# Sample attention of a decoder step: keys turned by VectorE in 32 by 32 blocks, scores in sixteen array tiles, pages loaded across sequences

## The chip, the core and the metric

The kernel runs on one core of a Trainium2 chip. The metric is device microseconds from launch to end, with the median of the runs as the kernel's time.

## The reference, cut to what matters

Layer 1 of the trunk attends with stick breaking. The change touches only the sample group: 8 sequences of 8 new tokens each, 16 heads of 64, and 4096 cached keys and values in 32 pages of 128 rows. A page of keys is 128 rows of 1024 fp32 numbers, 512 KB, and so is a page of values; 512 pages are read, 268 MB.

```python
def _stick_breaking(q, k, v, q_pos0, break_bias):
    ...
        z = jnp.einsum('bqhd,bkhd->bhqk', qb, kb) * scale + bias
        mask = kpos[None, :] < qpos[:, None]
        log_beta = jax.nn.log_sigmoid(z)
        log_keep = jnp.where(mask, log_beta - z, 0.0)
        rest = lax.cumsum(log_keep, axis=3, reverse=True) - log_keep
        a = jnp.where(mask, jnp.exp(log_beta + rest), 0.0)
        outs.append(jnp.einsum('bhqk,bkhd->bqhd', a, vb))
```

So each key's weight needs the sum of softplus(z) over all later keys. The kernel goes through the pages from the last to the first and subtracts that sum from z by matmuls with a triangular matrix.

## The kernel before

The program is a list of stages, each a block of its own: setup, pooling mixer, MLP, projections, `attend_sample` (the stage changed), `attend_prompt`, projection, MLP, norms. Every engine has its own in-order stream of instructions inside a stage; semaphores tie them together.

`attend_sample` first handles the 64 new keys (front part, up to the exponential of `zn` into `att_new`). Then comes a loop over the 8 sequences (`Fori(0, DB)`), with 8 units each; a unit is 4 pages. In a unit TensorE does, in this order:

1. `turn_keys(u)`: 32 transposes of 128 by 128 turn 4 pages of keys into PSUM, four banks in rotation. ScalarE and VectorE copy every other bank to `k_t` (`keep_turned`).
2. `scores(u)`: 8 matmuls, each with 32 query columns as weights and 512 keys streaming, on the four column tiles of the array. Each fp32 matmul stands in the profile as two MATMUL instructions.
3. `subtract_sums(u-1)`: 10 fp32r matmuls.
4. `turn_scores(u)`: 4 transposes of the biased scores `z_rows`, which VectorE made from the bank `Z`.
5. `values(u-1)`: 16 matmuls, on the four column tiles.

ScalarE takes abs, exp and ln of the turned scores (`t`), and later the exponential that gives the weights `att`. VectorE makes the softplus `sp` and its two fp32r halves `sp_hi`, `sp_lo`; GpSimd keeps `behind`, the sum over the pages already done. At a sequence's end the last `subtract_sums` and `values` run alone, VectorE picks each head's block of the result, and only then does the next sequence's first `scores` start.

SyncE issues the page loads in order: 4 pages of keys of unit u (two buffers of 4 pages, each waits until the page that it overwrites has been turned), then 4 pages of values of unit u-1 (8 slots, they wait on `v_used`). Its first key load waits on `k_turned`, which TensorE raises only after the new keys' part.

Of the kernel before, what the change touches and what calls it, by code (L numbers as in the profile page):

```python
# [16 lines left out]
ALU = mybir.AluOpType  # L17
ACT = mybir.ActivationFunctionType
AX = mybir.AxisListType
# [90 lines left out]
def setup(nc, k, a):  # L110
    with ExitStack() as ctx:
# [39 lines left out]
        def _(pool):  # L151
            def made_by(ins):
# [12 lines left out]
            made_by(pool.tensor_copy(k.neg_ones[:, :], k.scratch[:, :]))  # L165
# [9 lines left out]
            made_by(pool.memset(k.scratch[:, :], 0.0))  # L175
            made_by(pool.affine_select(out=k.scratch[:, :], in_=k.scratch[:, :], compare_op=ALU.is_gt, fill=MASKED,
                                       base=0, pattern=[[1, P]], channel_multiplier=-1))
            made_by(pool.tensor_copy(k.mask_diag[:, :], k.scratch[:, :]))
# [19 lines left out]
        MADE = 19 + HIST  # L198
# [752 lines left out]
def attend_sample(nc, k, a):  # L951
# [4 lines left out]

    with ExitStack() as ctx:
        o = k.HH_AT
        k_t = k.at("sa_kt", [P, NC, 512], F32, o)
        k_pages = [k.at("sa_kpage0", [P, 4, D], F32, o + 16384), k.at("sa_kpage1", [P, 4, D], F32, o + 51712)]  # L960
        z_rows = k.at("sa_zrows", [P, 512], F32, o + 32768)
        t = k.at("sa_t", [P, 512], F32, o + 34816)
        spl = k.at("sa_sp", [P, 4, P], F32, o + 36864)
        sp_hi = k.at("sa_sphi", [P, 2, 4, P], F32R, o + 38912)
        sp_lo = k.at("sa_splo", [P, 2, 4, P], F32R, o + 43008)
        behind = k.at("sa_behind", [P, P], F32, o + 47104)
        behind_hi = k.at("sa_behindhi", [P, 2, P], F32R, o + 47616)
        q_tiles = k.at("sa_q", [P, NC, 32], F32, o + 49152)
        o_part = k.at("sa_op", [P, 4, HD], F32, o + 50176)
        o = k.WORK_AT  # L970
        v_page = k.at("sa_vpage", [P, 8, D], F32, o)
        k_new = k.at("sa_knew", [P, D], F32, o + 32768)
        v_new = k.at("sa_vnew", [P, D], F32, o + 36864)
        att = k.at("sa_a", [P, 2, 512], F32, o + 40960)
        behind_lo = k.at("sa_behindlo", [P, 2, P], F32R, o + 45056)
        pages2 = k.at("sa_pages2", [P, 2, P], F32, o + 46080)
        att_new = k.at("sa_anew", [P, DB, P], F32, o + 47104)
        sp_new = k.at("sa_spnew", [P, DB, P], F32, o + 51200)
        o_rows = k.at("sa_or", [P, DB, P], F32, o + 55296)
        att_b = k.at("sa_ab", [P, P], F32, o + 59392)  # L980

        o = k.HH_AT
        zn = k.at("sa_zn", [P, DB * P], F32, o)
        spn_hi = k.at("sa_spnhi", [P, DB * P], F32R, o + 4096)
        spn_lo = k.at("sa_spnlo", [P, DB * P], F32R, o + 8192)
        tn = k.at("sa_tn", [P, DB * P], F32, o + 12288)
        kn_t = k.at("sa_knt", [P, NC, P], F32, o + 32768)
        (zeroed, kn_in, vn_in, kn_turned, kn_kept, zn_part, zn_done, zn_kept, tn_own, tn_done, dve_new, spn_done, trin_done,
         an_done, k_turned, act_kept, dve_kept, z_done, z_kept, zt_done, act_own, t_done, s_done, sp_done, behind_done,
         pool_own, tri_done, a_done, ab_done, v_used, o_row, o_turned, dve_own, q_ready) = sems(  # L990
            ctx, nc, "sa", "zeroed", "kn_in", "vn_in", "kn_turned", "kn_kept", "zn_part", "zn_done", "zn_kept", "tn_own",
            "tn_done", "dve_new", "spn_done", "trin_done", "an_done", "k_turned", "act_kept", "dve_kept", "z_done",
            "z_kept", "zt_done", "act_own", "t_done", "s_done", "sp_done", "behind_done", "pool_own", "tri_done",
            "a_done", "ab_done", "v_used", "o_row", "o_turned", "dve_own", "q_ready")
# [3 lines left out]
        UNITS = 8  # L998
        TURNS = 64
        Z, ZTS, OA = k.ps[3], [k.ps[4], k.ps[6]], k.ps[5]  # L1000
        ZN = [k.ps[5], k.ps[6]]
        OT = [k.ps[6], k.ps[3]]
        TURN_BANKS = [k.ps[0], k.ps[1], k.ps[2], k.ps[7]]
        npages = a["cache_k"].shape[0]

# [3 lines left out]
        @block.sync  # L1009
        def _(sp):  # L1010
            kc = a["cache_k"].rearrange("n p h d -> n p (h d)")
            vc = a["cache_v"].rearrange("n p h d -> n p (h d)")
            sp.wait_ge(zeroed, 2)
            sp.dma_start(k_new[0:TS, :], a["k_sample"].rearrange("b t h d -> (b t) (h d)")).then_inc(kn_in, 16)
            sp.dma_start(v_new[0:TS, :], a["v_sample"].rearrange("b t h d -> (b t) (h d)")).then_inc(vn_in, 16)
            with sp.Fori(0, DB) as b:

                page = {}
                for u in range(UNITS + 1):
                    for g in range(4 if u < UNITS else 0):  # L1020
                        n = 4 * u + g
                        page[n] = sp.value_load(k.pages[0:1, bass.ds(b * PAGES + (PAGES - 1 - n), 1)],
                                                min_val=0, max_val=npages - 1)

                        sp.wait_ge(k_turned, b * TURNS + (2 * (n + 25) if n < 8 else 2 * (n - 7) + TURNS))
                        sp.dma_start(k_pages[u % 2][:, g, :], kc[bass.ds(page[n], 1), :, :].rearrange("n p d -> (n p) d")
                                     ).then_inc(k_in[n % 8], 16)
                    for g in range(4 if u else 0):
                        n = 4 * (u - 1) + g
                        sp.wait_ge(v_used, b * UNITS + (u + 6))  # L1030
                        sp.dma_start(v_page[:, n % 8, :], vc[bass.ds(page[n], 1), :, :].rearrange("n p d -> (n p) d")
                                     ).then_inc(v_in[n % 8], 16)

        @block.gpsimd
        def _(pool):
            pool.memset(k_new[:, :], 0.0).then_inc(zeroed, 1)
            pool.memset(v_new[:, :], 0.0).then_inc(zeroed, 1)
            pool.memset(o_rows[:, :, :], 0.0).then_inc(zeroed, 1)

            own = Tally(pool, pool_own)  # L1040
            OWN = 2 + 7 * 4
            pool.wait_ge(spn_done, 1)
            pool.wait_ge(an_done, 1)
            with pool.Fori(0, DB) as b:
                own.base, own.k = b * OWN, 0
                for u in range(UNITS):
                    hi, lo = behind_hi[:, u % 2, :], behind_lo[:, u % 2, :]
                    pool.wait_ge(s_done, b * UNITS + (u + 1))
                    pool.wait_ge(behind_done, b * UNITS + u)
                    if u == 0:  # L1050
                        own.do(pool.tensor_tensor(behind[:, :], sp_new[:, bass.ds(b, 1), :].rearrange("p b n -> p (b n)"),
                                                  k.zeros[:, :], ALU.add))
                    else:
                        own.do(pool.tensor_tensor(pages2[:, :, :], spl[:, 0:2, :], spl[:, 2:4, :], ALU.add))
                        own.do(pool.tensor_tensor(pages2[:, 0, :], pages2[:, 0, :], pages2[:, 1, :], ALU.add))
                        own.do(pool.tensor_tensor(behind[:, :], behind[:, :], pages2[:, 0, :], ALU.add))
                    own.do(pool.tensor_tensor(hi, behind[:, :], k.zeros[:, :], ALU.add))
                    pool.tensor_tensor(lo, behind[:, :], hi.bitcast(F32), ALU.subtract).then_inc(behind_done, 1)
                    if u == 0:
                        pool.wait_ge(ab_done, b)  # L1060
                        pool.tensor_tensor(att_b[:, :], att_new[:, bass.ds(b, 1), :].rearrange("p b n -> p (b n)"),
                                           k.zeros[:, :], ALU.add).then_inc(ab_done, 1)
                assert own.k == OWN, own.k

        def keep_turned(eng, copy, mine, b, u, kept, pages):

            for g in pages:
                for h in range(2):
                    job = 8 * u + 2 * g + h
                    if job % 2 != mine:  # L1070
                        continue
                    eng.wait_ge(k_turned, b * TURNS + (TURNS + job + 1))
                    eng.wait_ge(z_done, b * UNITS + (u + 1))
                    copy(k_t[:, 4 * h:4 * h + 4, g * P:(g + 1) * P],
                         TURN_BANKS[job % 4][:, :].rearrange("p (c n) -> p c n", c=4)).then_inc(kept, 1)

        @block.scalar
        def _(act):
# [13 lines left out]
            act.wait_ge(an_done, 1)  # L1092
            act.sem_inc(act_kept, 32)
            with act.Fori(0, DB) as b:
# [6 lines left out]
                for u in range(UNITS):  # L1101
                    keep(u, range(4))
                    if u:
                        weights(u - 1)
# [622 lines left out]
```

## Time and profile before

| | |
|---|---|
| median of 3 runs | 3733.98 us (3733.38 to 3736.93) |
| profiled execution | 3737.79 us |
| its span | 3736.1 us |
| busy in the span | PE 86%, PE weight load 73%, DVE 50%, ACT 25%, POOL 16% |
| mean granted TensorE clock | 0.946 of 2.4 GHz |
| packets of the page loads | 4096 bytes each, 128 to a page |

The profile gives for each engine what it did and what ended its idle time. A stage is read with a view of stretches (busy time by engine, granted clock as PEclk with 1.00 for 2.4 GHz and 0.50 for 1.2 GHz, DMA rate) and with the timeline, whose rows give a start, a duration and a number of merged instructions.

### The profile page before, as it was taken

The numbers are of one execution on the slowest core, as the hardware profiler recorded it, in microseconds if no ns is written. First come the engines' busy times: TensorE is split into PE (matmuls) and PEld (weight loads), VectorE is DVE, ScalarE is ACT, GpSimd is POOL, SyncE is SP. The second block draws the span as 40 slices with busy tenths as digits, with TensorE's granted clock in tenths as the row PEclk, the third lists the DMA queues.
The fourth block names the chain that finished last, engine by engine and source line by source line (L and its number), as shares of the span: only waits on it lengthen the run. The fifth ranks groups of instructions, "written<-read, shape, count | busy, mean of one in ns | idle before, by whom it ended". The sixth has DMA issues, their size and how long they took to land. (4 is left out here: it accounts for less than half of the span.)

```text
span 3736.1 us, 57991 instructions
## 1 busy us (share of the span) xinstructions
PE 3210.8 (86%) x20912; PEld 2718.3 (73%) x20912; DVE 1885.8 (50%) x3138; ACT 937.8 (25%) x1598; POOL 610.8 (16%) x528
## 2 busy tenths in 40 slices
PE   5655999999995979788888887888885999999997
PEld 1235999999985979555555555444484999999996
DVE  2566555555543121344444444888815555555554
ACT  0113000000012010333333333777714100000003
POOL 0002222212101111122222221000010222222210
PEclk7887999999997989899999998999997999999998
DMA  8702111111101220798888886000010211111101
GB/s 323 261 29 62 46 45 45 40 43 42 39 0 58 88 63 26 284 351 341 337 350 334 340 339 225 22 19 23 6 45 0 68 45 45 45 45 45 45 22 48
DMA packets 215604, 432.70 MB, mean 116 GB/s; under 512 B 13664, under 2 KB 130057, under 8 KB 212441
## 3 DMA queue, kind: packets, MB, share of 16 engines
q1 hardware_dynamic: 215521, 431.67, 31.7%
q8 instruction: 43, 0.70, 0.1%
q14 instruction: 40, 0.33, 0.0%
HBM read 417.92 MB, written 13.92 MB: 116 GB/s over the span
## 5 line engine op out<-in xcount | busy, mean ns | idle before, releaser
L84 PE MATMUL bank<-hi,mlp_uphi 128*128 128x364 f32 (+1 forms) x1536 | 506.9, 330 | 92.2 <-POOL mlp_uplo L697 92.2
L85 PE MATMUL bank<-lo,mlp_uphi 128*128 128x364 f32 (+1 forms) x1536 | 506.7, 330 | 0.0
L86 PE MATMUL bank<-hi,mlp_uplo 128*128 128x364 f32 (+1 forms) x1536 | 506.6, 330 | 0.0
L85 PE MATMUL bank<-mlp_flo,mlp_dnhi 128*128 128x364 f32 (+1 forms) x1536 | 504.7, 329 | 0.0
L86 PE MATMUL bank<-mlp_fhi,mlp_dnlo 128*128 128x364 f32 (+1 forms) x1536 | 504.7, 329 | 0.0
L84 PE MATMUL bank<-mlp_fhi,mlp_dnhi 128*128 128x364 f32 (+1 forms) x1536 | 504.6, 329 | 0.0
L307 DVE SCALAR_TENSOR_TENSOR x_t<-bank,mod,x_t 128x364 f32<-128x364 f32 (+1 forms) x432 | 245.5, 571 | 379.7 <-PE bank L86 377.4
L84 PEld LDWEIGHTS bank<-hi,mlp_uphi 128*128 128x128 f32 x1536 | 290.5, 189 | 93.4 <-POOL mlp_uplo L697 93.4
L697 POOL TENSOR_TENSOR mlp_uplo<-mlp_raw,mlp_uphi 128x1024 fp32r<-128x1024 f32 x64 | 162.5, 2540 | 827.3 <-ACT mlp_uphi L682 423.3
L85 PEld LDWEIGHTS bank<-lo,mlp_uphi 128*128 128x128 f32 x1536 | 290.5, 189 | 0.0
L86 PEld LDWEIGHTS bank<-hi,mlp_uplo 128*128 128x128 f32 x1536 | 290.3, 189 | 0.0
L86 PEld LDWEIGHTS bank<-mlp_fhi,mlp_dnlo 128*128 128x128 f32 x1536 | 288.7, 188 | 0.0
L85 PEld LDWEIGHTS bank<-mlp_flo,mlp_dnhi 128*128 128x128 f32 x1536 | 288.7, 188 | 0.0
L84 PEld LDWEIGHTS bank<-mlp_fhi,mlp_dnhi 128*128 128x128 f32 x1536 | 288.7, 188 | 0.0
L697 POOL TENSOR_TENSOR mlp_dnlo<-mlp_raw,mlp_dnhi 128x1024 fp32r<-128x1024 f32 x64 | 163.2, 2550 | 673.7 <-ACT mlp_dnhi L682 673.7
L1249 PEld LDWEIGHTS bank<-ident,sa_kpage 128*128 128x128 f32 x2048 | 225.6, 142 | 44.6 <-issue 24.7
L1249 PE MATMUL bank<-ident,sa_kpage 128*128 128x128 f32 x2048 | 247.4, 277 | 12.0 <-ACT sa_kt L1100 6.0
L682 ACT ACTIVATE mlp_dnhi<-mlp_raw 128x1024 fp32r<-128x1024 f32 x64 | 67.4, 1053 | 750.7 <-PE bank L86 656.1
L718 DVE TENSOR_SCALAR mlp_f<-bank 128x364 f32<-128x364 f32 (+1 forms) x192 | 102.2, 532 | 234.7 <-PE bank L86 234.7
L722 DVE TENSOR_TENSOR mlp_flo<-mlp_f,mlp_fhi 128x364 fp32r<-128x364 f32 (+1 forms) x192 | 198.4, 1033 | 6.6
L682 ACT ACTIVATE mlp_uphi<-mlp_raw 128x1024 fp32r<-128x1024 f32 x60 | 63.7, 1061 | 534.5 <-PE bank L86 534.5
L84 PE MATMUL bank<-kv_hi,hi 128*128 128x256 f32 (+1 forms) x576 | 163.4, 284 | 38.1 <-POOL kv_lo L820 38.1
(255 smaller groups left out, 5652.7 us busy)
## 6 DMA issues: line engine op xcount, KB each, us to landing
sa_kpage<-in_cache_k SPq DMA_DIRECT2D x256, 512.0 KB, 6.4
sa_vpage<-in_cache_v SPq DMA_DIRECT2D x256, 512.0 KB, 6.1
mlp_raw<-in_w_up SPq DMA_DIRECT2D x64, 512.0 KB, 4.0
mlp_raw<-in_w_down SPq DMA_DIRECT2D x64, 512.0 KB, 3.5
w_raw<-in_w_ada SPq DMA_DIRECT2D x24, 1024.0 KB, 8.6
pm_wada<-in_w_ada SPq DMA_DIRECT2D x48, 512.0 KB, 5.2
kv_raw<-in_w_kv SPq DMA_DIRECT2D x8, 1024.0 KB, 5.5
x_rows<-in_x_prompt SPq DMA_DIRECT2D x1, 4096.0 KB, 13.4
```

The source lines that it names most:

```text
L84: pe.matmul(out, w_hi, x_hi, start=start, stop=False, skip_group_check=True)
L85: pe.matmul(out, w_hi, x_lo, start=False, stop=False, skip_group_check=True)
L86: return pe.matmul(out, w_lo, x_hi, start=False, stop=stop, skip_group_check=True)
L307: dve.scalar_tensor_tensor(out=x, in0=psum[:, 0:wp], scalar=g[:, 8 * gate + m, 0:1], in1=x, op0=ALU.mult, op1=ALU.add).then_inc(free, 1)
L682: act.activation(split_target(kind, c)[0], raw[:, r % 2, :], ACT.Copy).then_inc(w_hi_done, 1)
L697: pool.tensor_tensor(lo, raw[:, slot, :], hi.bitcast(F32), ALU.subtract).then_inc(w_done, 1)
L718: own.do(dve.tensor_scalar(ft, u, 0.0, None, ALU.max))
L722: dve.tensor_tensor(f_lo[:, c, c0:c0 + w], ft, hi.bitcast(F32), ALU.subtract).then_inc(bank_free, 1)
L1249: last = pe.transpose(TURN_BANKS[job % 4][:, c * P:(c + 1) * P], k_pages[u % 2][:, g, (4 * h + c) * P:(4 * h + c + 1) * P], k.ident[:, :])
```

## The change

`attend_sample` is rewritten around other units of work, and its loop over sequences is unrolled on all engines but SyncE, which loops over the first seven sequences.

- `turn_keys` moves to VectorE: one `dve.transpose` per page (128 partitions, 1024 elements) turns each 32 by 32 block in place, SBUF to SBUF. The copies on ScalarE and VectorE go.
- `scores` takes 128 matmuls of 32 rows, 32 weight columns and 128 keys, on the 16 tiles of the array, each row quarter into its own bank. The queries are laid out for this by `ready_queries`, 16 small copies per sequence on VectorE.
- ScalarE adds the bias: 4 activations of 128 columns make `z_rows`.
- `values(n-1)` stands between `scores(n+1)` and `turn_scores(n+1)`; `subtract_sums(n)` is last and has 6 matmuls in place of 10, because VectorE keeps a running sum `c_run` (4 adds of 128 columns per unit). GpSimd's part shrinks to the new keys.
- Units are numbered through the sequences (n from 0 to 63); two PSUM banks `OA` alternate between sequences, and `finish(b)` runs inside the next sequence.
- SyncE issues keys of unit n+1, then values of unit n, without a break between sequences, and the first keys may load before the new keys' part is done. In setup the constants `neg_ones` and `mask_diag` go.

The core of the diff:

```diff
+            def load_keys(b, u):
+                for g in range(4):
+                    page[4 * u + g] = page_of(b, 4 * u + g)
+                    sp.wait_ge(turned, b * (4 * UNITS) + (4 * u + g - 7 + EARLY_K))
+                    sp.dma_start(k_raw[u % 2][:, g, :], ...).then_inc(k_in[4 * (u % 2) + g], 16)
+            def load_values(b, u):
+                for g in range(4):
...
+                    sp.wait_ge(v_used, b * UNITS + (u - 1 + EARLY_V))
+                    sp.dma_start(v_page[:, 4 * (u % 2) + g, :], ...).then_inc(v_in[4 * (u % 2) + g], 16)
...
+            def softplus_of_negative(n):
+                act.wait_ge(z_done, n + 1)
+                act.wait_ge(zt_done, n)
+                for r in range(4):
+                    act.activation(z_rows[:, :, r, :],
+                                   Z[r][:, P * (n % 2):P * (n % 2) + P].rearrange("p (x j) -> p x j", j=32),
+                                   ACT.Identity, bias=k.bias_row[:, 0:1]).then_inc(z_kept, 1)
...
+            def turn_keys(n, x):
...
+                dve.wait_ge(k_in[4 * (n % 2) + x], 16 * (n // 2 + 1))
+                dve.transpose(k_t[n % 2][:, x, :], k_raw[n % 2][:, x, :]).then_inc(turned, 1)
...
+            for n in range(W):
+                dve.wait_ge(l_done, n + 1)
+                dve.scalar_tensor_tensor(flat, ZT[n % 2][:, :], 0.0, flat, ALU.max, ALU.add).then_inc(sp_done, 1)
...
+                for g in range(4):
...
+                    dve.tensor_tensor(c_run[:, g, :], before, t[:, g, :], ALU.add).then_inc(c_done, 1)
...
+                dve.tensor_copy(c_hi[:, n % 2, :, :], c_all).then_inc(hi_done, 1)
+                dve.tensor_tensor(c_lo[:, n % 2, :, :], c_all, c_hi[:, n % 2, :, :].bitcast(F32), ALU.subtract
+                                  ).then_inc(lo_done, 1)
+                for x in range(4):
+                    turn_keys(n + 2, x)
+                if u == 1 and b:
+                    finish(b - 1)
+                if 2 <= u < 6 and b + 1 < DB:
+                    ready_queries(b + 1, u - 2)
...
+            def scores(n):
+                pe.wait_ge(turned, EARLY_K + 4 * n + 4)
...
+                for hh in range(4):
+                    for half in range(2):
+                        for r in range(4):
+                            for g in range(4):
+                                d0 = HD * (4 * g + hh) + 32 * half
+                                last = pe.matmul(
+                                    Z[r][32 * g:32 * g + 32, P * (n % 2):P * (n % 2) + P].rearrange("p (x j) -> p x j", j=32),
+                                    q_w[b % 2][32 * r:32 * r + 32, g, half, 32 * hh:32 * hh + 32],
+                                    k_t[n % 2][32 * r:32 * r + 32, :, d0:d0 + 32], ...
+                                    tile_position=(32 * r, 32 * g), skip_group_check=True)
...
+            for n in range(W):
+                if n + 1 < W:
+                    scores(n + 1)
+                if n:
+                    values(n - 1)
+                if n + 1 < W:
+                    turn_scores(n + 1)
+                subtract_sums(n)
```

## Rows read from the trace of the kernel before

**Rows 1.** The page's first line.

```profile
span 3736.1 us, 57991 instructions
```

**Rows 2.** Stretches: the loop over the sequences, with the columns' names.

```profile
core 0: us, PE busy (x) PEld busy (x) DVE busy (x) ACT busy (x) POOL busy (x), PEclk, DMA share, GB/s
...
1524.40:2309.60 785.20, 657.39 (x6080) 449.23 (x6080) 343.74 (x559) 302.52 (x512) 183.28 (x312) 0.98 0.88 341
```

**Rows 3.** Timeline of one unit: start us, us, engine, line, operation [idle before].

```profile
1598.57 1.92 PE L1262 MATMUL bank<-sa_kt,sa_q 128*32 128x512 f32 x16 [1.25 <-issue]
...
1600.42 0.50 PE L1287 MATMUL bank<-sa_sphi,neg_tri 128*128 128x512 f32 x1
...
1602.26 0.60 PE L1271 MATMUL bank<-ident,sa_zrows 128*128 128x128 f32 x4
...
1603.11 1.93 PE L1294 MATMUL bank<-sa_vpage,sa_a 128*32 128x256 f32 x32 [0.25 <-ACT sa_a L1097]
...
1604.97 3.72 PE L1249 MATMUL bank<-ident,sa_kpage 128*128 128x128 f32 x32
...
1608.21 4.05 SPq L1026 DMA_DIRECT2D sa_kpage<-in_cache_k  x4
...
1609.93 1.92 PE L1262 MATMUL bank<-sa_kt,sa_q 128*32 128x512 f32 x16 [1.25 <-issue]
```

**Rows 4.** Timeline at a sequence's end and the next one's first scores.

```profile
1621.05 1.93 PE L1294 MATMUL bank<-sa_vpage,sa_a 128*32 128x256 f32 x32 [0.69 <-ACT sa_a L1097]
...
1628.30 1.92 PE L1262 MATMUL bank<-sa_kt,sa_q 128*32 128x512 f32 x16 [1.06 <-DVE sa_kt L1074]
```

**Rows 5.** Stretches: page loads saturated, setup, and the first 75 us of the loop.

```profile
1562.00:1592.00 30.00, 25.51 (x236) 17.41 (x238) 13.41 (x21) 11.49 (x20) 7.19 (x13) 1.00 1.03 408
...
50.00:70.00 20.00, 11.83 (x72) 1.81 (x68) 1.00 (x2) 0.00 (x0) 0.00 (x0) 0.82 1.01 421
...
1524.40:1600.00 75.60, 63.91 (x578) 44.53 (x578) 34.87 (x57) 30.13 (x51) 19.55 (x34) 0.97 1.01 400
```

**Rows 6.** Groups of instructions in the loop: count, busy us, mean ns, idle before.

```profile
L1180 DVE TENSOR_TENSOR sa_splo<-sa_sp,sa_sphi 128x512 fp32r<-128x512 f32 x64 | 55.8, 872 | 0.3
...
L1174 DVE SCALAR_TENSOR_TENSOR sa_sp<-bank,sa_t 128x512 f32<-128x512 f32 x64 | 44.3, 692 | 223.7 <-ACT sa_t L1112 223.7
...
L1108 ACT ACTIVATE sa_t<-bank 128x512 f32<-128x512 f32 x64 | 37.9, 592 | 34.8 <-PE bank L1271 34.8
...
L1177 DVE CAST sa_sphi<-sa_sp 128x512 fp32r<-128x512 f32 x64 | 31.9, 498 | 0.3
```

**Rows 7.** Timeline: VectorE over 1024 elements, the new keys' last softplus half.

```profile
1518.54 1.23 DVE L1130 TENSOR_TENSOR sa_spnlo<-sa_spnew,sa_spnhi 128x1024 fp32r<-128x1024 f32 x1
```

**Rows 8.** One line's instructions: VectorE's reduction over 256, ns min/median/max.

```profile
L1188 DVE TENSOR_REDUCE sa_or<-sa_op x8: 585/610/618, 1623.7 to 2310.3; 128x256 f32 x8
```

**Rows 9.** Groups over 128 columns on VectorE and ScalarE, in `attend_prompt`.

```profile
L1499 DVE TENSOR_TENSOR pa_crun<-pa_crun,pa_t 128x128 f32<-128x128 f32 x32 | 7.7, 283 | 0.0
...
L1437 ACT ACTIVATE pa_t<-bank 128x128 f32<-128x128 f32 x24 | 6.6, 275 | 3.7 <-DVE bank L1487 3.7
```

**Rows 10.** Timeline: matmuls on two row halves; weight loads for four column tiles.

```profile
2343.94 1.13 PE L1540 MATMUL bank<-q_t,pa_kt 64*128 64x512 f32 x4
...
1545.88 0.16 PEld L1294 LDWEIGHTS bank<-sa_vnew,sa_ab 128*32 128x32 f32 x8 [0.17 <-issue]
```

**Rows 11.** Stretch: the new keys' part, just before the loop.

```profile
1495.00:1524.00 29.00, 17.49 (x78) 15.00 (x78) 6.41 (x8) 4.51 (x5) 0.00 (x0) 0.50 0.10 30
```

**Rows 12.** Stretch: 200 us of `attend_prompt`, whose code is unrolled.

```profile
2400.00:2600.00 200.00, 167.56 (x792) 87.75 (x792) 169.50 (x350) 153.86 (x359) 7.62 (x8) 0.97 0.07 22
```

**Rows 13.** TensorE's code queue, 2400 to 2600, then 1545.5 to 1546.6: packets, MB, share.

```profile
q8 instruction: 6, 0.10, 0.2%
...
q8 instruction: 1, 0.02, 5.9%
```

**Rows 14.** Timeline: the stage's last instructions.

```profile
2311.61 3.52 DVE L1195 COPY o_s<-bank 64x32 f32<-64x32 f32 x32 [0.75 <-PE bank L1326]
```

More of the change, by code:

```diff
@@ L965, in attend_sample @@
[L965 to L969, printed above, removed]
+        k_raw = [k.at(f"sa_kraw{s}", [P, 4, D], F32, o + 16384 * s) for s in range(2)]
+        k_t = [k.at(f"sa_kt{s}", [P, 4, D], F32, o + 32768 + 16384 * s) for s in range(2)]
+        kn_t = k.at("sa_knt", [P, NC, P], F32, o + 32768)
@@ L1015, in _, with page_of @@
             sp.dma_start(v_new[0:TS, :], a["v_sample"].rearrange("b t h d -> (b t) (h d)")).then_inc(vn_in, 16)
-            with sp.Fori(0, DB) as b:
-                page = {}
[L1019 to L1032, printed above, removed]
+            def page_of(b, n):
+                return sp.value_load(k.pages[0:1, bass.ds(b * PAGES + (PAGES - 1 - n), 1)], min_val=0, max_val=npages - 1)
@@ new lines, in _ @@
+            page = {}
+            load_keys(0, 0)
+            with sp.Fori(0, DB - 1) as b:
+                page = {}
+                for u in range(UNITS):
+                    if u + 1 < UNITS:
+                        load_keys(b, u + 1)
+                        load_values(b, u)
+                    else:
+                        kept = dict(page)
+                        load_keys(b + 1, 0)
+                        page = kept
+                        load_values(b, u)
+            page = {}
@@ L1034, in _ @@
+            for u in range(UNITS):
+                if u + 1 < UNITS:
+                    load_keys(DB - 1, u + 1)
+                load_values(DB - 1, u)
         @block.gpsimd
@@ L1037, in _ @@
             pool.memset(v_new[:, :], 0.0).then_inc(zeroed, 1)
[L1038 to L1075, printed above, removed]
+            for s in range(2):
+                pool.memset(q_w[s][:, :, :, :], 0.0).then_inc(q_zeroed, 1)
@@ L1130, in _, with ready_queries @@
             dve.tensor_tensor(spn_lo[:, :], sp_flat, spn_hi[:, :].bitcast(F32), ALU.subtract).then_inc(spn_done, 1)
+            dve.tensor_reduce(sp_all[:, :], sp_new[:, :, :].rearrange("p b n -> p n b"), AX.X, ALU.add).then_inc(summed, 1)
+            def ready_queries(b, g):
+                if b == 0 and g == 0:
+                    dve.wait_ge(q_zeroed, 2)
+                if b >= 2:
+                    dve.wait_ge(z_done, UNITS * (b - 1))
+                rows = slice(32 * g, 32 * g + 32)
+                for par in range(2):
+                    for half in range(2):
+                        src = 64 * par + 32 * half
+                        dve.tensor_copy(
+                            q_w[b % 2][rows, :, half, :].rearrange("p g (h s) -> p g h s", h=4)[:, :, par::2, 0:DS],
+                            k.q_t[src:src + 32, :, TP + b * DS:TP + b * DS + DS].rearrange("p (g r) q -> p g r q", r=2)
+                            ).then_inc(q_ready, 1)
+            for g in range(4):
+                ready_queries(0, g)
             dve.wait_ge(trin_done, 1)
@@ new lines, in turn_scores, with subtract_sums @@
+            def turn_scores(n):
+                pe.wait_ge(z_kept, 4 * n + 4)
+                if n >= 2:
+                    pe.wait_ge(a_done, n - 1)
+                for x in range(4):
+                    last = pe.matmul(ZT[n % 2][:, P * x:P * x + P], z_rows[:, x, :, :].rearrange("p r j -> p (r j)"),
+                                     k.ident[:, :], start=(x == 0), stop=False, is_transpose=True, skip_group_check=True)
+                last.then_inc(zt_done, 1)
+            def subtract_sums(n):
+                b, u = divmod(n, UNITS)
+                zt = ZT[n % 2][:, :].rearrange("p (g n) -> p g n", g=4)
+                pe.wait_ge(lo_done, n + 1)
+                if u == 0:
+                    pe.wait_ge(new_ready, 2 * b + 1)
+                for half, new in ((c_hi, pn_hi), (c_lo, pn_lo)):
+                    pe.matmul(zt, k.neg_tri[:, :], half[:, n % 2, :, :], start=False, stop=False, skip_group_check=True)
+                    pe.matmul(zt[:, 1:4, :], k.neg_above[:, :], half[:, n % 2, 0:3, :], start=False, stop=False,
+                              skip_group_check=True)
+                    last = pe.matmul(zt[:, 0, :], k.neg_above[:, :], half[:, 1 - n % 2, 3, :] if u else new[:, :],
+                                     start=False, stop=(half is c_lo), skip_group_check=True)
+                last.then_inc(tri_done, 1)
@@ new lines, in add_values, with values @@
+            def add_values(b, weight, v, start, stop):
+                for q in range(4):
+                    last = pe.matmul(OA[b % 2][32 * q:32 * q + 32, 0:4 * HD], weight[:, 32 * q:32 * q + 32],
+                                     v[:, 256 * q:256 * q + 256], start=start, stop=stop,
+                                     tile_position=(0, 32 * q), skip_group_check=True)
+                return last
+            def values(n):
+                b, u = divmod(n, UNITS)
+                if u == 0:
+                    pe.wait_ge(new_ready, 2 * b + 2)
+                    pe.wait_ge(vn_in, 16)
+                    if b >= 2:
+                        pe.wait_ge(o_part_done, b - 1)
+                    add_values(b, att_b, v_new, True, False)
+                pe.wait_ge(a_done, n + 1)
+                for g in range(4):
+                    slot = 4 * (n % 2) + g
+                    pe.wait_ge(v_in[slot], 16 * (n // 2 + 1))
+                    last = add_values(b, att[:, g, :], v_page[:, slot, :], False, u == UNITS - 1 and g == 3)
+                last.then_inc(v_used, 1)
@@ L1324, in _ @@
+            scores(0)
+            turn_scores(0)
+            for n in range(W):
+                if n + 1 < W:
+                    scores(n + 1)
+                if n:
+                    values(n - 1)
+                if n + 1 < W:
+                    turn_scores(n + 1)
+                subtract_sums(n)
+            values(W - 1)
+            pe.wait_ge(o_row, DB)
             for j in range(2):
                 for b in range(4):
-                    last = pe.transpose(OT[j][:, b * P:(b + 1) * P], o_rows[:, 4 * j + b, :], k.ident[:, :])
+                    last = pe.transpose(OT[j][0:HD, b * P:(b + 1) * P], o_rows[:, 4 * j + b, :], k.ident[:, :])
```

335 lines of the change are left out of this document (134 added, 201 removed).

## The prediction

> **What bounds the kernel now.** I read the page first, then the stretches of each stage, then one unit of the changed stage in the timeline, then the groups there.
>
> The whole span is 3736.1 us [rows 1]. The loop over sequences takes 785.2 of it [rows 2], TensorE is busy 657.4 us of that, and the loads move 341 GB/s on average. From this row alone either could be the limit.
>
> The timeline decides. A unit is 11.36 us from `scores` to `scores` (1598.57 to 1609.93) and TensorE goes through it almost without a gap: scores 1.92, `subtract_sums` 1.84 (1600.42 to 1602.26), turned scores and values to 1604.97, then 3.7 us of key transposes, and a last wait of 1.25 us in which the copies of the turned keys end [rows 3]. So inside a sequence the order of work on TensorE sets the pace. Between sequences there is more: the scores of the last unit start at 1609.93 and those of the next sequence at 1628.30, 18.4 us, with the last values standing alone at 1621.05 [rows 3, 4]. That is 7.0 more than a unit, eight times 56. 64 x 11.36 = 727, and with the 56 nearly all of the 785 is told.
>
> Are loads a limit too? Where many are queued they run at 408 GB/s, and at 421 in setup [rows 5]. A unit loads 8 pages, 4.194 MB: at 408 GB/s 10.28 us. That is the floor close beneath the 11.36: whatever TensorE saves beyond 1.1 us a unit is not gained.
>
> **The change, engine by engine, per unit.**
>
> *TensorE.* Out: 3.7 us of transposes and the 1.25 us wait behind them. `subtract_sums` streams 2 x (512+384+128) = 2048 columns in 6 matmuls, before 3584 in 10 in 1.84 us, so 1.05 to 1.10; I take 1.2. Values (1.93) and turned scores (0.60) stay [rows 3].
> The new scores are 128 matmuls, 256 MATMUL rows of 128 columns. The old ones are 16 rows of 512 columns, four side by side, in 1.92 us. Per place in the array the work is equal if sixteen run side by side (256 x 128 / 16 = 16 x 512 / 4 = 2048): 1.9 us. If only four do, 4 x 1.92 = 7.7 us. What speaks for sixteen: one round of four old scores takes 1.92 / 4 = 0.48 us; in `attend_prompt` four matmuls of 512 columns on two row halves took 1.13 us, two rounds and a tail, not four rounds of 1.92, so row parts do overlap. And eight weight loads of 32 columns took 0.16 us together, the last one's own time included, so issue holds 256 pairs to at most 256 x 20 ns = 5.1 us and likely much less [rows 10]. I take 2.2, ends 1.9 and 7.7.
> Sum: 2.2 + 1.93 + 0.60 + 1.2, and 0.4 for four waits, 6.3 us.
> The Trainium skill (TensorE: Matmul & The Clock Gate, "Wait — 56ns, not 53.3ns?") says that starts of matmuls are never closer than about 25 ns. By it the scores would take 256 x 25 ns = 6.4 us, an estimate from that page, and TensorE's unit 10.5 us, level with the loads (rival 1). The rows of weight loads stand closer than 25 ns, but they are not matmuls.
>
> *VectorE.* Out: four copies and the bias. In: softplus 0.69, halves 0.50 and 0.87 [rows 6], 4 adds of 0.28 [rows 9], 4 page turns, 0.4 for the waits between dependent steps (estimate). No row has a turn. Nearest: 128 x 1024 fp32 elements in one pass, 1.23 us [rows 7]; dear end: the reduction, 0.61 for 256, four times that, 2.4 us [rows 8]. A turn reads and writes each element once, as the first does, so I take 1.23. Sum: 3.6 + 4 x 1.23 = 8.5 us, and in four units of a sequence up to 4 x 0.28 for queries, 9.6. Cover is the 10.4 of the loads; it is gone at 1.7 us a turn.
> The Trainium skill (Vector Engine (DVE) Microarchitecture Reference, 3.8) has the 32 by 32 turn sustain one element per cycle and lane; by it the sum is the one taken. No row here shows it.
>
> *ScalarE.* Four evictions at 0.275 and four passes at 0.6 [rows 6, 9]: 3.5 us, hidden. `z_rows` (1.1 us) lie under `values` (1.93); were they not, turned scores would come up to 1.1 later, still within the slack below.
>
> *GpSimd* leaves the unit.
>
> *Loads.* SyncE issues four key pages in 4.05 us [rows 3]; values are no dearer, so at most 8.1 a unit, below 10.3. One wait heads each batch of 8 pages: values n+2 wait for `values(n)`, and keys n+4 are queued behind them. Is the batch issued before the one ahead has drained? When keys n+3 have landed: turn 1.25, scores 2.2, values 1.93, semaphores 0.3, so 5.7 us later the wait opens, while the next batch needs 10.3 us to drain. 4.6 us spare; the queue does not run dry. The sequence's end no longer interrupts it.
> *Code.* The unit now has 604 TensorE instructions (2 x 256, 2 x 32, 8, 12 and some 8 waits), unrolled 64 times, 38,700. In `attend_prompt` 1584 of them go with 6 blocks, 264 a block [rows 12, 13]: some 146 blocks, 2.3 a unit. A block takes 5.9% of sixteen engines for 1.1 us, 1.04 us of one engine [rows 13]. Spread over the sixteen: 0.15 us a unit. On one: 2.4. I take the spread, since the first 75 us of the loop, where the old loop loads its own code once, still ran at 400 GB/s [rows 5].
>
> So the loads are the longest: 10.28 + 0.15 = 10.43 us a unit, against 9.6, 6.3 and 3.5.
>
> **The sum over the stage.**
> Start. The softplus half of the new keys ends at 1519.8 [rows 7]. Then one reduction (1.6, between 1.23 and 2.4), 16 small copies (3.0, estimated at 0.19 each, under the 0.28 of 128 columns), the bias, exponential and second reduction (4.0), four turns (5.0): first scores near 1533.6. Units 0 to 2 are paced by what hangs on what: scores(0) 2.2, bias 1.1, turned scores 0.7, ScalarE 2.1, VectorE 3.3 until 1543.0, then the turns of unit 2 (5.0) until 1548.1, scores(2) 2.2 and `values(0)` until 1552.2. Keys of units 0 to 3 and values 0 and 1 are long under way, the first of them since before the new keys' part. At 1552.2 the wait opens for values 2 and keys 4, which land, some 3.5 us from issue to the first landing and 7 pages of 1.28 later, at 1564.7.
> Middle. Keys 4 to keys 63: 59 x 10.43 = 615.4, to 2180.1.
> Tail. Turn 1.25, scores 2.2, `values(61)` 1.9, turned scores 0.7, ScalarE 2.1, VectorE 3.3, subtract 1.3, exponential 0.7, values 2.1, pick and reduce 1.1, transposes 1.2, copies 3.5 [rows 14]: 21.6, to 2201.7.
> Before, the stage's last copy ends at 2315.1 [rows 14]. Gain 113.4 us. The profiled execution took 3737.8 us; it becomes 3624.4. It lies 3.8 above the median of 3734.0, so on the median: 3620.6. What comes before and after is untouched; setup's two constants are off the path.
> Own range: at 421 GB/s 59 x 0.32 less, 3602; at 400 and a fill 7 us longer, 3640.
>
> **The rivals.**
> 1. *TensorE at the low clock.* In the stretch before the loop TensorE was busy 17.5 of 29 us and the granted clock 0.50, which is 1.2 GHz [rows 11]; in the loop it is 0.98 [rows 2]. With 6.3 of 10.4 us busy, it may fall. At that level scores, values and turned scores double (from 1.9, 1.93 and 0.6) and the subtract grows to some 1.9: 3.8 + 3.9 + 1.2 + 1.9 + 0.4 = 11.2. With TensorE as the bound the end is the first scores, 64 units and a last 9.5 us: 1533.6 + 64 x 11.2 + 9.5 = 2260, time 3679; then busy again, it would rise, so somewhere from 3625 to 3679. Against: 0.82 at a similar share in setup [rows 5]. Slow issue of the scores ends alike: at 6.4 us of scores the unit is 10.5, the end 2215, the time 3634, and it is counted here. (The skill's 25 ns would be this case.)
> 2. *Only four score tiles at a time.* 7.7 + 1.93 + 0.6 + 1.2 + 0.4 = 11.8; the end by the same sum 2298, the time 3717. Against: the two halves overlap [rows 10].
> 3. *VectorE is the bound.* Turn of T us: unit 3.6 + 4T, from T = 1.7 it binds, at 2.1 the unit is 12.0 and all is lost, at 2.4 it is 13.2 and the time, by the sum of rival 1, some 3807.
> 4. *Slower: code on one load engine.* If every block of TensorE's code goes by the same of the sixteen engines, each page waits for that one: 10.28 + 2.4 = 12.7 a unit, 59 x 2.25 = 133 us more, 3753. It decides from about four blocks in five on one engine. For it: blocks do take one engine's time [rows 13], and the loop before loads its code once, so it had few. Against: the 400 GB/s above.
> 5. *The pages do not run on*: if SyncE's order stops the queue at each unit, as it does now (341 GB/s), the stage stays at the old rate: 268.4 MB / 341 = 787 us, no change. The 4.6 us spare speak against it.
>
> **How the numbers follow.** Forecast 0.58. Rival 1 0.17, rival 2 0.06, rival 3 0.08 (half of it faster), rival 4 0.06, rival 5 0.02, other waits 0.03. The time is the forecast's: 3621 us. Its own range is 3600 to 3640. The range 3600 to 3700 takes in rival 1 and the cheap part of rival 3, near 0.8. A difference under 0.2%, 7 us, is no change here. Faster: 0.58 + 0.17 + 0.06 + 0.04 + 0.03 = 0.88; same 0.03; slower 0.09 (rivals 3 and 4).
>
> **What would show it.** In the stretches of the loop: 400 GB/s or more, PE near 6 to 7 of 10.4 us per unit, VectorE near 8.5. A `scores` group of 256 rows spanning 2 us, a turn of 1.2 us. VectorE's turns should be waiting for the pages' DMA, and SyncE for `values` only briefly. PEclk under 0.8 with no DMA wait shows rival 1, scores of 6 to 8 us rival 2, no idle VectorE rival 3, a rate under 350 GB/s with all engines waiting for pages rival 4, the same with SyncE waiting rival 5. The prediction is wrong if an engine is busy without a pause while the loads are not.

## The result: 4.0% slower

After the change the median is 3888.3 us of 4 runs (3875.9 to 3891.2); the kernel before on the same chip took 3735.5 (3733.4 to 3737.1). The ratio is 1.040, with a 95% interval of 1.038 to 1.043. The forecast was 3621, range 3600 to 3700.

The page of the changed kernel, its first line and TensorE's code queue (packets, MB, share of the load engines' time):

```profile
span 3888.5 us, 81895 instructions
...
q8 instruction: 187, 3.06, 0.3%
```

The span is 152.4 us longer than that of [rows 1]. Two stretches of the changed kernel: one inside the sample stage, then all that comes before it (columns as in [rows 2]):

```profile
core 0: us, PE busy (x) PEld busy (x) DVE busy (x) ACT busy (x) POOL busy (x), PEclk, DMA share, GB/s
1600.00:2100.00 500.00, 325.88 (x10185) 215.95 (x10185) 284.61 (x455) 118.70 (x272) 6.74 (x16) 0.78 0.77 288
...
0.00:1492.00 1492.00, 1267.96 (x7762) 1166.28 (x7762) 679.18 (x1062) 185.93 (x210) 229.81 (x122) 0.93 0.22 75
```

What comes before the stage is as it was, within 2 us of TensorE's busy time. The kernel before in the same stretch:

```profile
0.00:1492.00 1492.00, 1269.87 (x7762) 1166.51 (x7762) 679.22 (x1062) 185.99 (x210) 228.66 (x126) 0.93 0.22 75
```

The stage's last copy, which ended at 2315.1 before [rows 14], in the timeline of after:

```profile
2470.75 3.51 DVE L1221 COPY o_s<-bank 64x32 f32<-64x32 f32 x32 [1.16 <-PE bank L1339]
```

It ends at 2474.3, 159 us later, so the stage holds the whole loss (what follows gave back 7 us, which I did not trace). In the stage nothing is full: the loads run at 288 GB/s where [rows 2] have 341, TensorE is busy 326 of 500 us, VectorE 285. No engine and no queue is busy without a pause, so some wait sets the pace.

The groups of the changed kernel that cost most in the stage (count, busy us, mean ns, idle before and its cause), from its page:

```profile
L1272 PE MATMUL bank<-sa_kt,sa_q 32*32 32x128 f32 x16384 | 286.1, 316 | 291.9 <-issue 257.9
...
L1169 DVE STREAM_TRANSPOSE sa_kt<-sa_kraw 128x1024 f32<-128x1024 f32 x256 | 313.9, 1243 | 285.3 <-DMA sa_kraw<-in_cache_k 270.1
```

A page turn takes 1.243 us, the 1.23 of the forecast. Ahead of the scores TensorE idles 292 us, 258 of it with the mark "issue": it waits for nothing that a semaphore shows. The timeline shows the form of it, here the scores of two units (start us, us, engine, line, operation, [idle before]):

```profile
2005.76 1.82 PE L1272 MATMUL bank<-sa_kt,sa_q 32*32 32x128 f32 x118
...
2008.68 1.89 PE L1272 MATMUL bank<-sa_kt,sa_q 32*32 32x128 f32 x128 [1.10 <-issue]
...
2015.72 0.66 PE L1272 MATMUL bank<-sa_kt,sa_q 32*32 32x128 f32 x10 [5.14 <-issue]
...
2021.06 2.82 PE L1272 MATMUL bank<-sa_kt,sa_q 32*32 32x128 f32 x202
...
2028.70 1.43 PE L1272 MATMUL bank<-sa_kt,sa_q 32*32 32x128 f32 x54 [4.82 <-issue]
```

There is no wait in the code inside the 256 matmuls of a unit's scores, yet they break off. The piece between two gaps at 2008.68, 128 matmuls each with its weight load, is 256 instructions, about the 264 a block that the prediction counted from [rows 12, 13]. The code queue in four stretches there, 2005.9 to 2018.6, 2005.9 to 2007.5, 2013 to 2015 and 2017.3 to 2018.8:

```profile
q8 instruction: 3, 0.05, 1.7%
...
q8 instruction: 1, 0.02, 4.7%
...
q8 instruction: 1, 0.02, 3.0%
...
q8 instruction: 1, 0.02, 5.2%
```

Between 2007.5 and 2013 no block comes, and the scores resume at 2015.72, after the one that starts in 2013 to 2015. (The block's packet is recorded at 2013.44 and takes 0.98 us.) In 1600 to 2100 the loads' queue and the code queue of after:

```profile
q1 hardware_dynamic: 39211, 142.78, 76.1%
q8 instruction: 81, 1.33, 1.0%
```

That is one block per 6.17 us. Page turns in the same stretch are 136, four a unit, so the unit is 500 x 4 / 136 = 14.7 us, and 81 / 34 = 2.4 blocks go with each. The forecast had 2.3.

The theories for the experiments:
- **Theory 1**: TensorE goes through its written-out code faster than blocks of it arrive. One comes about every 6.1 us beside the page loads; 604 / 256 = 2.36 of them a unit make 14.4 us.
- **Theory 2**: the page queue. Keys are issued behind values, which wait for TensorE's `values`, and this round trip sets the pace.
- **Theory 3**: the scores' matmuls take long in themselves, at the granted clock of 0.78.

### The profile page after: what moved, and what is told of

The parts are those of the page before. It is cut to its first block and busy times, and to the rows that moved or that the text cites. A ratio compares the mean times of both kernels' runs of the same rounds, so it can differ in the third digit from the quotient of the medians.

```text
span 3888.5 us, 81895 instructions
## 1 busy us (share of the span) xinstructions
PE 3172.5 (82%) x33968; PEld 2682.1 (69%) x33968; DVE 2078.1 (53%) x3427; ACT 858.2 (22%) x1598; POOL 443.8 (11%) x248
## 5 line engine op out<-in xcount | busy, mean ns | idle before, releaser
L1272 PE MATMUL bank<-sa_kt,sa_q 32*32 32x128 f32 x16384 | 286.1, 316 | 291.9 <-issue 257.9
L1169 DVE STREAM_TRANSPOSE sa_kt<-sa_kraw 128x1024 f32<-128x1024 f32 x256 | 313.9, 1243 | 285.3 <-DMA sa_kraw<-in_cache_k 270.1
L1272 PEld LDWEIGHTS bank<-sa_kt,sa_q 32*32 32x32 f32 x16384 | 222.4, 112 | 339.1 <-issue 278.1
L1305 PE MATMUL bank<-sa_vpage,sa_a 128*32 128x256 f32 x2048 | 217.6, 579 | 22.8 <-issue 20.6
```

Of the source, the lines that this page charges most:

```text
L1169: dve.transpose(k_t[n % 2][:, x, :], k_raw[n % 2][:, x, :]).then_inc(turned, 1)
L1272: last = pe.matmul(Z[r][32 * g:32 * g + 32, P * (n % 2):P * (n % 2) + P].rearrange("p (x j) -> p x j", j=32), q_w[b % 2][32 * r:32 * r + 3 ...
L1305: last = pe.matmul(OA[b % 2][32 * q:32 * q + 32, 0:4 * HD], weight[:, 32 * q:32 * q + 32], v[:, 256 * q:256 * q + 256], start=start, stop= ...
```

## The experiments

In the table the unit is worked out as above, from the page turns in 1600 to 2100; "us a block" is 500 over the blocks of the code queue there, and the last column is the time in us that TensorE stood with the mark "issue" ahead of or within scores in the same 500 us. "Keys ahead" is the edit of the first experiment. The kernels with a part of the scores off or with light pages leave work out: they are no versions to be used, and their times serve to tell the theories apart.

| kernel | time, us | ratio to before | unit, us | blocks | us a block | PE waits on issue, scores |
|---|---|---|---|---|---|---|
| after | 3888.3 | 1.040 | 14.71 | 81 | 6.17 | 144.1 |
| keys ahead | 3870.8 | 1.037 | 14.29 | 82 | 6.10 | 145.1 |
| control, written out | 3944.8 | 1.057 | 15.50 | 77 | 6.49 | 135.2 |
| the same, looped | 3701.1 | 0.991 | 11.36 | 1 | | none |
| looped, keys ahead | 3642.3 | 0.975 | 10.47 | 1 | | none |
| a quarter of scores off | 3768.0 | 1.009 | 12.82 | 73 | 6.85 | 64.2 |
| half off | 3671.2 | 0.984 | 11.11 | 60 | 8.33 | none |
| quarter off, keys ahead | 3712.5 | 0.995 | 11.70 | 78 | 6.41 | 100.5 |
| half off, keys ahead | 3628.8 | 0.972 | 10.64 | 63 | 7.94 | 2.5 |
| light pages | 3643.6 | 0.976 | 10.42 | 113 | 4.42 | 73.9 |
| light pages, keys ahead | 3622.1 | 0.970 | 9.95 | 117 | 4.27 | 75.9 |
| before, written out | 3727.1 | 0.999 | | 32 | 15.6 | 39.0 |

### Keys ahead of values

```diff
             load_keys(0, 0)
+            load_keys(0, 1)
...
-                    if u + 1 < UNITS:
-                        load_keys(b, u + 1)
+                    if u + 2 < UNITS:
+                        load_keys(b, u + 2)
                         load_values(b, u)
...
-                        load_keys(b + 1, 0)
+                        load_keys(b + 1, u + 2 - UNITS)
```

> Nothing changes but SyncE's order: the keys of unit n+2 are issued before the values of unit n, so that a batch of keys no longer stands behind the wait for TensorE's values. Theory 1 (TensorE waits for blocks of its unrolled code, 2.36 blocks a unit at about 6.2 us each): the unit stays at 14.0 to 14.6 us and the kernel at 3860 to 3900. Theory 2 (the cycle of the page queue sets the pace, values wait ahead of keys): the unit falls towards the loads' 10.43 to 11.5 us and the kernel to 3640 to 3720. Theory 3 (TensorE's dear scores at a low clock): the unit stays above 14 too, but TensorE's waits with the mark issue would not be what fills it.

3870.8 us, ratio 1.037 (1.035 to 1.039). Waits of this kernel in 1600 to 2100 (us in total, times, longest):

```profile
PE bank L1273 <- issue: 145.1, 38, 6.0
```

VectorE no longer waits for a page at all (in after it did for 157.5 us of this stretch), and still the unit is 14.29 us. The pages are there, and the issue waits are as long as before (145.1 and 144.1 us). Theory 2 is out as the main cause; the order is worth 17.6 us of time here. That the missing thing is code is shown by the next pair of kernels.

### TensorE's code in a loop, and its control

TensorE's part is put as two units, `pair(b, i)`, either written out 31 times (the control) or in a loop (four pairs in each of seven sequences, three in the last); what stands before the first pair and behind the last is written out in both. A body that serves every unit needs one query tile and one output bank, and the new keys' sums copied to where the carry stands. TensorE also gets one more semaphore instruction ahead of each unit's scores and waits at a sequence's start until the last result is picked. Cut to what matters:

```diff
+                if u == 0:
+                    dve.tensor_copy(c_hi[:, 1, 3, :], pn_hi[:, :]).then_inc(pn_kept, 1)
...
+                if u == UNITS - 2 and b + 1 < DB:
+                    for g in range(4):
+                        ready_queries(b + 1, g)
...
-                if u == 1 and b:
+                if u == 0 and b:
                     finish(b - 1)
...
+            def pair(b, i):
+                base = b * 8 + i * 2
+                for d in (1, 2):
+                    scores(base + (d + 1), (d + 1) % 2)
+                    values(base + (d - 1), b * 4 + i, (d - 1) % 2)
+                    turn_scores(base + (d + 1), (d + 1) % 2)
+                    subtract_sums(base + d, d % 2)
...
+            with pe.Fori(0, DB - 1) as b:        # control: for b in range(DB - 1)
+                start_sequence(b)
+                with pe.Fori(0, 4) as i:         # control: for i in range(4)
+                    pair(b, i)
```

> A control for the next kernel, with the code still unrolled: one query tile and one output bank in place of two, the new keys' sums copied into the carry's place, the queries of a sequence turned in one go, one semaphore instruction more ahead of each unit's scores. All theories: the unit stays at 14.2 to 15, the kernel at 3860 to 3940, with one block of TensorE's code fetched per 6.2 us.

> The control with TensorE's instructions for two units in a loop, in place of the 64 units written out; same work, order and waits. Theory 1: almost no blocks of code are fetched in the stage (under 20 in the place of some 150), TensorE's issue waits go from about 260 us to under 40, the unit falls to 10.6 to 11.8 us (loads at 10.43, or the cycle of turn 1.25, scores 3.8, values 3 and a batch of loads of 15), the kernel to 3640 to 3730. Theory 2: the unit stays above 13.5, the kernel above 3830. Theory 3 (scores of 3.8 us at a low clock by themselves): 13 to 14 us, 3790 to 3860.

The control took 3944.8 us (1.057, 1.055 to 1.059), a little above its range, and so is its unit, 15.50 us: these changes to the body together cost 56 us on top of after. The loop and the control differ in three lines, the `for` or `Fori` of TensorE. In the loop the same work took 3701.1 (0.991, 0.989 to 0.993). The looped kernel in 1600 to 2100, the stretch:

```profile
1600.00:2100.00 500.00, 361.23 (x13252) 277.40 (x13236) 365.80 (x602) 154.67 (x356) 8.41 (x20) 0.82 0.95 368
```

Its code queue there:

```profile
q8 instruction: 1, 0.02, 0.0%
```

And what the scores wait for there:

```profile
PE bank L1281 <- DVE sa_kt L1171: 101.7, 31, 5.7
```

One block in 500 us, no issue wait of the scores' matmuls, and the scores now wait for page turns. The loop is worth 3944.8 - 3701.1 = 244 us, 4.1 us a unit. The granted clock moved little (0.73 in the control, 0.82 in the loop) and the scores' matmuls are the same, so theory 3 is out as the main cause, too.

### The loop with keys ahead

> Both: TensorE's loop and the keys ahead of the values in SyncE's order. Theory 1: 10.43 to 11.0 us a unit, the loads' floor, 3630 to 3680; against the loop alone it shows what the order of the page queue costs once the code is there (0 to 1 us a unit). Theory 2: the same time here, but then the keys ahead alone would have given it. Theory 3: above 13 us still.

3642.3 us (3638.2 to 3643.6), ratio 0.975 (0.973 to 0.977): the fastest version that leaves nothing out, 93 us under the kernel before and 246 under the change. Its stretch:

```profile
1600.00:2100.00 500.00, 384.44 (x14079) 293.67 (x14068) 392.48 (x640) 165.50 (x379) 10.08 (x24) 0.83 1.01 400
```

The load engines are full. The unit is 10.47 us; the forecast had 10.43. So the page queue's order does cost, 0.9 us a unit and 59 us in all, but only once the code is there; while TensorE waits for code it costs 17.6.

### Fewer instructions, code written out

A quarter of the scores' matmuls left out, or half (the sum over a head is then short of these terms):

```diff
                             for g in range(4):
+                                if half and r >= 2:      # half off: if half
+                                    continue
```

> The changed kernel, code still unrolled, with a quarter of the scores' matmuls left out (part of the sum over each head is missing): 476 instructions a unit in place of 604, 1.86 blocks in place of 2.36. Theory 1 (blocks of code come at 6.2 us each and TensorE waits for them): 1.86 x 6.2 = 11.5, so 11.5 to 12.2 us a unit, 3700 to 3760. Theory 3 (the matmuls' own time): a quarter of 3.8 us less, about 13.5 us a unit, 3810 to 3830.

> The same with half of the scores' matmuls left out: 348 instructions a unit, 1.36 blocks. Theory 1: 1.36 x 6.2 = 8.4 us, under the loads' 10.3, so the loads and the order of the page queue bind: 10.4 to 11.5 us a unit, 3630 to 3700. Theory 3: about 12.5 us a unit, 3750 to 3770.

A quarter off: 3768.0, unit 12.82, above theory 1's 12.2 and below theory 3's 13.5. Half off: 3671.2, unit 11.11, within theory 1's 10.4 to 11.5. The first is no clean answer, since code and page queue both hold it: in 500 us there are 64 us of issue waits and 139 of waits for pages. So both again, with keys ahead:

> Keys ahead of values and a quarter of the scores' matmuls left out, code unrolled: 1.86 blocks a unit. With the page queue's own cycle out of the way, the law of theory 1 (unit = blocks times 6.1 us, or the loads' 10.4 if longer) gives 11.35: 11.2 to 11.8 us a unit, 3680 to 3720, where the same omission with values ahead of keys measured 12.8 us and 3768. If what is left over there was not the page queue, it stays at 12.5 to 12.8 and near 3760.

> The same with half of the scores' matmuls left out: 1.36 blocks, 8.3 us by the law, so the loads bind: 10.4 to 10.6 us a unit, 3630 to 3650 (values ahead of keys: 11.1 and 3671). A unit above 10.8 speaks against the law.

The group of page turns of the quarter-off kernel with keys ahead, in 1600 to 2100:

```profile
L1170 DVE STREAM_TRANSPOSE sa_kt<-sa_kraw 128x1024 f32<-128x1024 f32 x171 | 198.3, 1214 | 2.7 <-DMA sa_kraw<-in_cache_k 2.6
```

Its code queue:

```profile
q8 instruction: 78, 1.28, 1.0%
```

3712.5 us, unit 11.70 (the law gave 11.35), and 3628.8, unit 10.64 (the loads' 10.4). With the queue's order out of the way, the longer of two terms, blocks by 6.1 us or the loads' 10.4, gives 14.4, 11.3, 10.4 where 14.3, 11.7, 10.6 were measured for 604, 476, 348 instructions. Both shorter ones lie 0.2 to 0.4 us above it (half off was expected at 10.4 to 10.6), so the law is a good estimate and not exact.

### Is a block asked for only when it is missed?

The kernel before with TensorE's loop over sequences written out:

```diff
-            with pe.Fori(0, DB) as b:
+            for b in range(DB):
```

> The kernel before, with TensorE's loop over the sequences written out and nothing else changed: some 190 instructions a unit, 0.73 block, one block per 16.8 us of the old pace. Theory 1a (blocks come one at a time but ahead of TensorE, so only their rate of one per 6.2 us limits): no change, 3730 to 3750. Theory 1b (each block is asked for when TensorE reaches its end, and TensorE stands 3 to 5 us each time): 47 blocks by 3 to 5 us, less what the waits between units absorb, 3820 to 3970.

3727.1 us, ratio 0.9988 (0.9979 to 0.9998): no loss, where theory 1b had 3820 or more. Its code queue in 1600 to 2100:

```profile
q8 instruction: 32, 0.52, 0.4%
```

And its scores' issue wait there:

```profile
PE bank L1262 <- issue: 39.0, 31, 1.4
```

One block per 15.6 us passes without a wait; the kernel before, with its loop, has 39.3 us in the same row. So blocks are fetched ahead of use (theory 1a), and what counts is how fast they can follow each other. Writing code out cost nothing here; it cost 244 us where 256 instructions run shorter than a block takes.

### What sets the time of a block?

Only columns 0 to 255 of each page are loaded, keys and values; GpSimd sets the rest to zero ahead of them, so the unit is to be compared and not the kernel's time:

```diff
-                    sp.dma_start(k_raw[u % 2][:, g, :],
-                                 kc[bass.ds(page[4 * u + g], 1), :, :]
+                    sp.dma_start(k_raw[u % 2][:, g, 0:256],
+                                 kc[bass.ds(page[4 * u + g], 1), :, 0:256]
```

> The changed kernel with a quarter of each page loaded (256 of 1024 columns; the rest of the keys and values is zero), code still unrolled. Theory 1 with the block's time set by the queueing behind page loads: with the queues mostly idle a block takes well under 6.2 us, the issue waits shrink, and the unit falls to VectorE's and TensorE's own 8.5 to 10.5 us. If a block takes 6 us whatever the queues carry: still about 14 us a unit. Rival of the prediction (the loads slowed by the code on one load engine): the unit falls to 8.5 too, but then the issue waits would stay few in the changed kernel already, which they are not.

> Keys ahead of values, code unrolled, a quarter of each page loaded. The run with light pages had a block per 4.4 us and a unit of 10.4 with TensorE still waiting on issue 1.8 us a unit. If TensorE's code is what bound it (2.36 blocks at 4.4 us), the order makes no difference: 10.2 to 10.5 us a unit. If the page queue's cycle or VectorE bound it: 9.0 to 9.8 us.

Light pages in 1600 to 2100, the stretch:

```profile
1600.00:2100.00 500.00, 395.69 (x14456) 281.75 (x14431) 389.67 (x641) 167.44 (x384) 10.10 (x24) 0.91 0.34 105
```

The code queue there:

```profile
q8 instruction: 113, 1.85, 1.5%
```

And the scores' issue wait there:

```profile
PE bank L1275 <- issue: 73.9, 46, 2.4
```

With the load engines at 0.34 a block comes every 4.4 us in place of 6.2, and the mean gap ahead of scores is 1.6 us in place of 4.0 (144.1 / 36). So the page loads lengthen a block's time. The packet records say where: in after as in light pages a block's packet takes 1.0 us, and where a row of matmuls of one line had broken off for more than 0.8 us it goes on 1.4 us after the packet's end (medians; 40 and 49 such gaps in 1600 to 2100). What the loads add therefore lies ahead of the packet's start. That it stands there behind packets of pages is likely and not shown. The rest of a block's time is not the loads': with idle room on the engines TensorE still waits for code.

With keys ahead as well the unit is 9.95, between the two ranges expected (9.0 to 9.8, and 10.2 to 10.5), so code and the page order may both have had a part; the block's 4.27 times 2.36 is 10.1. The 4.3 is an upper bound for a block beside light loads, as TensorE's own work is close to this pace.

### One line moved in the best version

> The kernel with TensorE's loop and the keys ahead, with one line moved: at a sequence's first unit VectorE does the last sequence's pick and sum before the four page turns, not after them. In the run before TensorE waited for it 22.7 us in six sequences. Loads at 409 GB/s are the floor, so most of that is hidden already: 0 to 15 us faster than 3642, 3625 to 3645; at a floor of 10.25 us a unit not more.

```diff
+                if u == 0 and b:
+                    finish(b - 1)
                 for x in range(4):
                     turn_keys(n + 2, x)
-                if u == 0 and b:
-                    finish(b - 1)
```

3643.6 us, ratio 0.976 (0.9745 to 0.977): no difference. The 22.7 us that TensorE had waited at the sequences' starts are gone from its waits, and the one on page turns went from 92.2 us to the one of this row, so the time is only waited elsewhere; the loads run at 400 GB/s in both, with the load engines' share at 1.01, so they are the bound:

```profile
PE bank L1282 <- DVE sa_kt L1172: 120.4, 46, 5.0
```

## Why the prediction was wrong

**The step that failed** is "Code" under the loads. The count was right, 146 blocks at 2.3 a unit: the page of after has 187 in the code queue where that of before has 43. But a block was priced as the load engines' time alone, "spread over the sixteen: 0.15 us a unit", and checked only against the loads' rate. No sentence asked how long TensorE waits for a block. The same rows allowed the question: [rows 12, 13] have 6 blocks in 200 us, one per 33 us, with nearly idle load engines, so nothing there showed what happens at one per 4.4 us (10.43 / 2.36). The cost was unknown and should have had a bound; TensorE's wait was put at nothing. Measured: a block per 6.1 us beside page loads, so 14.3 to 14.7 us a unit, of which TensorE stands about 4 us without code ahead of or within the scores (257.9 / 64); the loop, which spares the blocks, gives back 4.1 us a unit. This is a wait of TensorE, not a load on the engines.

The Trainium skill (Runtime: NRT & Kernel Launch, "Instruction fetch mechanics") says that engines fetch code in blocks of 256 instructions ahead of use, that crossing a block is "mostly hidden", and that kernels prefer full unrolling. The kernel before agrees when written out (15.6 us a block, no added wait). The changed kernel does not: there a block is needed about every 4.4 us and the wait is 4 us at a time.

**Rival 4**, slower by code on one load engine (3753), has the right sign and subject, and the wrong mechanism: it needed pages to wait for a full load engine. The load engines were at 0.77, and with keys ahead no page turn waited for a page while the unit stayed at 14.3.

**Scores, 2.2 us**, were mis-sized. Two undisturbed ones of the looped kernel with keys ahead, in the timeline:

```profile
2004.76 5.40 PE L1282 MATMUL bank<-sa_kt,sa_q 32*32 32x128 f32 x256 [3.30 <-DVE sa_kt L1172]
...
2015.57 3.56 PE L1282 MATMUL bank<-sa_kt,sa_q 32*32 32x128 f32 x256 [1.48 <-DVE sa_kt L1172]
```

The stretches of the same times:

```profile
2004.76:2010.16 5.40, 5.40 (x260) 4.56 (x264) 2.62 (x7) 0.00 (x0) 0.00 (x0) 0.50 1.03 409
2015.57:2019.13 3.56, 3.56 (x260) 3.25 (x264) 2.72 (x7) 0.00 (x0) 0.00 (x0) 1.00 1.03 412
```

They take 3.56 us at the full clock and 5.40 at half of it. So at the full clock they are neither the 1.9 of sixteen tiles without overhead nor the 7.7 of four: 13.9 ns a matmul with its weight load. By the weight loads of [rows 10], 20 ns each, this was in reach (at most 5.1 us). The Trainium skill's floor of 25 ns between starts (TensorE: Matmul & The Clock Gate, "Wait — 56ns, not 53.3ns?") would make 6.4, an estimate from that page; the 3.56 measured does not agree, so the floor does not hold for these tiles.

**The clock (rival 1)** did fall, to 0.78 in after and 0.83 in the best version, but there the loads cover it: the unit is 10.47 with TensorE at that clock. Its condition came true in part and its price did not; the 11.2 us a unit were for the low clock throughout, which no run had.

**"4.6 us spare; the queue does not run dry"** failed with the code: with scores stretched to about 10 us by gaps, the values' wait opened too late: SyncE stood 250 of the 500 us for TensorE's `values`. With the code in a loop it is still 188 us and costs 0.9 us a unit. Scores of 3.6 to 5.4 in place of 2.2 take 1.4 to 3.2 of the 4.6 us. The rest is likely that the forecast's 5.7 us end when the wait opens: the issue and the 3.5 us to the first landing, which it has in its start, are missing there. How the 0.9 divides was not measured. Issuing keys first removes it (46 us of such waits).

**What held**: the turn of a page (1.23 forecast, 1.24 measured); VectorE (8.5 forecast, 392.48 x 4 / 191 = 8.2 in the best version); ScalarE, hidden; the loads' floor, 10.43 forecast and 10.47 measured, once two obstacles are gone; and nothing outside the stage lost. Two of the forecast's sums are off by 0.2 us, which changes nothing: the start's terms give 1533.4 and the tail's 21.35. From after to the best version the runs step as follows: 3888.3, plus 56.5 for the changes to the body, less 243.8 for the loop and 58.8 for the order, is 3642.2. The remaining 21 us to the forecast lie partly in the start: the first two units are written out in the best version too, and the timeline there has their scores end at 1544.4 and 1559.1, the first 8.6 us after the forecast's 1535.8. The rest I did not take apart.

## What to carry to other kernels

Count not only the bytes of written-out code but the time that 256 instructions of it last on their engine: here a block came per 4.3 us at most beside light loads and per 6.1 beside loads of 290 GB/s (at 400 GB/s no run shows the limit: half off with keys ahead needed one per 7.9 us and hardly waited). Code that runs through 256 instructions faster than that is paced by its own loading. Small tiles make this likely, since they turn the same work into more instructions; here such a body in a loop was 244 us faster. An idle time marked "issue" in the middle of a row of matmuls without a wait, with pieces of 128 matmuls and weight loads, is the sign of it.

## What was not expected of the hardware

- Code blocks come ahead of use, yet only one per 6.1 us beside page loads at about 290 GB/s (4.4 us at 105 GB/s), although the transfer itself takes 1.0 us of one load engine; the broken-off work goes on 1.4 us after its end.
- A matmul of a 32 by 32 tile with 128 columns and its weight load costs 13.9 ns over sixteen tiles at the full clock, and 21.1 at half: 1.5 times, less than the clock's ratio of 2, so part of it does not go by the granted clock.
